# A shorter plan for the second attention: 12 phases instead of 15, and its scaling on another engine

## The reference, cut to what matters

```python
h = rms_norm(x, mix_norm_g); proj = h @ w_in          # q, kv (3 branches), gate logits, conv input
k_cmp = compress_tokens(kv[:, :, 0, 0], ...)          # silu(flat @ w1) @ w2 on overlapping blocks of 32 tokens
v_cmp = compress_tokens(kv[:, :, 0, 1], ...)
# three attentions with a bias by distance: compressed keys, selected blocks, window of 512
p = masked_softmax(s + bias, valid)                   # each of the three
out = gc[..., 0:1] * o_cmp + gc[..., 1:2] * o_sel + gc[..., 2:3] * o_win
conv = silu(layer_norm(causal_depthwise_conv(a * sigmoid(gate), 31 taps)))
x = x + concatenate([attn, conv]) @ w_out
```

## Time and profile before

| what | us |
|---|---|
| median of 3 runs (range) | 2780.38 (2778.89 to 2782.11) |
| the profiled execution | 2782.15 |
| its span, first to last instruction | 2780.0 |
| TensorE busy | 2725.3 (98%) |
| VectorE busy | 1945.8 (70%) |
| ScalarE busy | 1405.2 (51%) |

### The profile page before, as it was taken

How to read it: one execution, slowest core, us unless ns; L and a number is a source line. 1 busy time by engine, 2 the same in 40 slices (tenths; PEclk the granted TensorE clock), 3 DMA queues, 4 the chain that set the end, 5 groups by cost and what they waited for, 6 DMA issues and landing times. The chain is left out here.

```text
span 2780.0 us, 41613 instructions
## 1 busy us (share of the span) xinstructions
PE 2725.3 (98%) x16606; PEld 2393.7 (86%) x16606; DVE 1945.8 (70%) x2922; ACT 1405.2 (51%) x2084; POOL 101.0 (4%) x189
## 2 busy tenths in 40 slices
PE   8999999999999999999999998998999999999998
PEld 7888888888888888888888898988888888888887
DVE  7448777757777775677666777876788775677765
ACT  6335555544455554455454551247555553455543
POOL 1320000000000000000000000000000000000000
PEclk9999999999999999999999999999999999999999
DMA  7457556555668788878656566762355556555554
GB/s 239 134 172 241 175 182 196 184 182 190 198 225 286 283 278 301 284 274 285 209 171 208 177 203 229 247 251 92 126 178 190 194 192 189 180 192 196 183 193 140
DMA packets 166609, 573.19 MB, mean 206 GB/s; under 512 B 19872, under 2 KB 26736, under 8 KB 165904
## 3 DMA queue, kind: packets, MB, share of 16 engines
q1 hardware_dynamic: 151216, 521.86, 56.5%
q0 software_dynamic: 15056, 48.65, 4.7%
q10 hardware_dynamic: 144, 0.01, 0.0%
HBM read 530.86 MB, written 38.90 MB: 205 GB/s over the span
## 5 line engine op out<-in xcount | busy, mean ns | idle before, releaser
L1902 DVE TENSOR_TENSOR wl<-raw,wh 128x1024 fp32r<-128x1024 f32 (+1 forms) x880 | 1029.3, 1195 | 448.5 <-ACT wh L1359 446.3
L1359 ACT ACTIVATE wh<-raw 128x1024 fp32r<-128x1024 f32 (+1 forms) x880 | 885.9, 1031 | 507.6 <-PE PS L947 420.0
L947 PE MATMUL PS<-CHt,wh 128*128 128x512 f32 x2816 | 886.1, 396 | 2.2 <-DVE wl L1902 2.2
L947 PE MATMUL PS<-BIGt,wh 128*128 128x512 f32 (+1 forms) x2816 | 756.9, 356 | 3.1 <-DVE wl L1902 2.0
L947 PEld LDWEIGHTS PS<-CHt,wl 128*128 128x128 f32 x2816 | 529.0, 188 | 124.8
L947 PE MATMUL PS<-AHt,wh 128*128 128x512 f32 (+1 forms) x1984 | 603.2, 385 | 12.0 <-DVE wl L1902 9.4
L947 PE MATMUL PS<-CHt,wl 128*128 128x256 f32 x2816 | 553.5, 278 | 0.0
L947 PEld LDWEIGHTS PS<-BIGt,wl 128*128 128x128 f32 x2304 | 435.5, 189 | 79.1 <-issue 0.2
L947 PE MATMUL PS<-BIGt,wl 128*128 128x256 f32 x2304 | 498.3, 279 | 0.0
L947 PEld LDWEIGHTS PS<-BIGt,wh 128*128 128x128 f32 x2816 | 435.1, 190 | 8.5 <-issue 5.2
L947 PEld LDWEIGHTS PS<-CHt,wh 128*128 128x128 f32 x2816 | 429.3, 189 | 2.7 <-issue 2.5
(11 more groups left out here) (307 smaller groups left out, 1659.0 us busy)
## 6 DMA issues: line engine op xcount, KB each, us to landing
raw<-in_w_up SPq DMA_DIRECT2D x264, 512.0 KB, 4.8
raw<-in_w_in SPq DMA_DIRECT2D x200, 512.0 KB, 4.0
raw<-in_w_down SPq DMA_DIRECT2D x132, 512.0 KB, 4.3
raw<-in_w_gate SPq DMA_DIRECT2D x88, 512.0 KB, 5.4
raw<-in_w_down SPq DMA_DIRECT2D x56, 384.0 KB, 3.5
raw<-in_w_ssd_br SPq DMA_DIRECT2D x32, 512.0 KB, 4.4
raw<-in_w_o SPq DMA_DIRECT2D x32, 512.0 KB, 4.2
PKR<-in_w_in SPq DMA_DIRECT2D x32, 512.0 KB, 5.4
```

Of the source, the lines that this page charges most:

```text
L947: return e.matmul(o, l, r, start=start, stop=stop, skip_group_check=True)
L1359: return e.activation(o, x, f, **k)
L1902: return e.tensor_tensor(o, x, y, op)
```

## The change

Three things change together. First, `ATTN2` has other numbers: 12 phases instead of 15. With 12 + 1 steps a stage, pairs 0 and 1 run in steps 1 to 12 and 3 to 14, and both are over before query unit 1 is finished (step 16). So pairs 2 and 3 start in the same step 17, pairs 4 and 5 in step 30, and 6 and 7 in step 43, and the parts of both stand side by side in each step, even pair first. The last one ends in step 54. Second, the four scalings of each branch go from ScalarE (phase `p0`/`p1`) to VectorE (in `scale`, phase `r0`/`r1`, right behind the reciprocals), and the transposes wait for VectorE instead. Third, phases 1 and 2 of each compression stage stand two pieces later: behind pieces 579 and 580 (key), 587 and 588 (value).

```diff
-ATTN2 = dict(sc0=0, cmp=2, tr0=5, o0=6, sc1=7, trc=10, oc=12, tr1=12, o1=14, s0=0, ca=2, r0=2, cb=5, s1=7, r1=9,
-             out=14, e0=2, ce=3, p0=3, t0=5, e1=9, tc=10, p1=10, t1=12)
+ATTN2 = dict(sc0=0, cmp=2, tr0=3, o0=5, sc1=5, trc=7, oc=8, tr1=8, o1=10, s0=0, ca=2, r0=2, cb=4, s1=5, r1=7,
+             out=11, e0=1, ce=3, t0=4, e1=6, tc=7, t1=9)
...
-            add("w_in_2", 0, 16, 1024 + 256 * i, "U2", "ev_cmp", i, gens=[("compress", i, [0, None, None, 1, 2])], **k)
+            add("w_in_2", 0, 16, 1024 + 256 * i, "U2", "ev_cmp", i, gens=[("compress", i, [0, None, None, None, None, 1, 2])], **k)
...
             if ph == ATTN2["tr0"]:
                 bank7("tr0")
-                e.wait_ge(ac.sem, ac.at(i, "p03"))
+                e.wait_ge(d.sem, d.at(i, "p03"))
                 e.wait_ge(d.sem, d.at(i, "cb1"))
...
             if ph == ATTN2["tr1"]:
                 bank7("tr1")
-                e.wait_ge(ac.sem, ac.at(i, "p13"))
+                e.wait_ge(d.sem, d.at(i, "p13"))
...
-            def scale(br):
-                e.wait_ge(d.sem, d.at(i, f"rg{br}1"))
-                for hh in range(2):
-                    for b, c0, c1 in HALVES:
-                        x = SX[:, hh, c0:c1]
-                        af(x, x, ACT.Copy, scale=RC[:, hh, b:b + 1]).then_inc(ac.sem)
...
                 for hh in range(2):
                     tt(RC[:, hh, :], RC[:, hh, :], GAT[:, :, 3 * (2 * t + hh) + 1 + br], MUL).then_inc(d.sem)
+                e.wait_ge(d.sem, d.at(i, f"rg{br}1"))
+                for hh in range(2):
+                    for b, c0, c1 in HALVES:
+                        x = SX[:, hh, c0:c1]
+                        ts(x, x, RC[:, hh, b:b + 1], None, MUL).then_inc(d.sem)
```

More of the change, by code:

```diff
@@ L710, in hybrid_block_kernel @@
     a2_d = [steps(f"attn2_d{u}", "n000", "n010", "n100", "n110", "cb0", "cb1", "cm", "cs0", "cs1", "cf", "rc0", "rg00",
[L711 to L714, removed]
+                  "rg01", *[f"p0{j}" for j in range(4)], "cd", "cr", "cc", "cg0", "cg1", "cx0", "cx1", "n001", "n011", "n101", "n111", "rc1", "rg10",
+                  "rg11", *[f"p1{j}" for j in range(4)]) for u in range(2)]
+    a2_a = [steps(f"attn2_a{u}", *[f"e0{i}" for i in range(4)], "ce", "pt0", *[f"e1{i}" for i in range(4)], "ptc", "pt1") for u in range(2)]
     add_d = steps("conv_half_added")
@@ L1764, in attn2 @@
                 af(SC[:, :, :, :], SC[:, :, :, :], ACT.Exp).then_inc(ac.sem)
-            if ph == ATTN2["p0"]:
-                scale(0)
             if ph == ATTN2["t0"]:
@@ L1774, in attn2 @@
                 af(PT[0:15, :, 0:256], PS[0:15, S0:S0 + 2, 0:256], ACT.Copy).then_inc(ac.sem)
-            if ph == ATTN2["p1"]:
-                scale(1)
             if ph == ATTN2["t1"]:
```

## The result

| kernel | median us (range, runs) | profiled execution | its span | mean clock |
|---|---|---|---|---|
| before | 2779.97 (2778.89 to 2782.11, 4) | 2782.15 | 2780.0 | 0.995 |
| after | 2797.51 (2796.26 to 2797.88, 4) | 2797.88 | 2796.1 | 0.990 |

The ratio is 1.0059 (95% interval 1.0047 to 1.0071): slower by 17.5 us. The forecast was 2791.0, +10.8. The sign was right and the time lies in the range of 2777 to 2802, but 0.5 us beyond the forecast's own range of 2785 to 2797; the clock rival's 2800 is nearer.

The account below looks back on a forecast made before the run. TensorE was taken as the bound, busy 2725.3 of 2780.0 us. Compression +3.7 and attention +7.1 (20.4 of waits plus 1.5 for clock, against 11.5 + 3.3) made +10.8: 2791.0 us, range 2777 to 2802.

Parts of the forecast that it names:

- the clock rival: TensorE: each wait of 3 us or more is followed by the lower clock level, +9, 2800 us; chance 19%.
- -0.8 for the clock: TensorE: +1 for piece 581 at half clock, +1.5 behind attention waits, against 3.3 lost before.
- Compression, forecast +3.7: Key and value products: token waits of 4.7 + 6.2 us replaced by 13.6 for halves and GCM, plus 1 for clock.
- the prediction's own list: Signs it is wrong: GCM before 582's split, 583's fetch earlier than 1683, or no transpose waits in pairs 4 to 7.
- Scaling, forecast 1.0 us a branch: Attention's four scalings on VectorE: 354 and 290 ns less 70 ns overlap each; bounds 0.75 and 1.4 us.
- Waits of the attention, forecast 20.4 us: TensorE's waits in lock step by pairs of pairs: 4.4 + 6 + 5 + 5 us, against 11.5 before.
- a lower clock behind one or two of them: Attention: 1.5 us for TensorE's lower clock behind one or two waits, against 3.3 before.
- The key product hidden as meant: Compression: VectorE isn't blocked, only the value side's 5.7 us go, 2781.6 us, no change; chance 8%.
- ScalarE as the bound: Stretch 1852 to 1907: ScalarE was the bound, a pair of pairs costs 1.5 instead of 5, 2776 us; chance 13%.
- Waits near half of mine: Waits near half of those forecast: 2783 to 2785 us, no change; chance 10%.

Follow-up runs that it names:

- attn_stagger: Changed kernel with the compression's phases as before and odd pairs two steps behind even ones, still 12 phases: 2785.65 us, +4.4 against before.
- scale_dve: Kernel before with only the scaling of the probabilities moved to VectorE, 15 phases and compression as before: 2781.52 us, ratio 0.9998.
- comp_only: Kernel before with only the compression's phases 1 and 2 two pieces later, key and value side: 2784.32 us, +3.0.
- key_one: Kernel before with the compression's key side one piece later and its value side two: 2783.09 us, ratio 1.0009.
- attn_only: Changed kernel with the compression's phases where they were before, so 12 phases, lock step and VectorE's scaling alone: 2795.85 us, +14.5 against before.
- fill_elsewhere: attn_only plus 43 useless TensorE products, all ahead of pair 7's last value product, behind its wait: 2804.22 us, +22.9 against before.
- fill_half: attn_only plus 43 useless TensorE products ahead of its waits for the scaled probabilities: 2787.18 us, +6.3 against before.
- lock_act: Kernel before with 12 phases and both pairs in step as in the change, ScalarE still scaling, compression as before: 2799.89 us, +18.5.
- bias_late: Kernel before with the value side's phases two pieces later and the attention's bias load issued one unit later: 2777.62 us, ratio 0.9988.
- value_fill: Kernel before with the value side's phases two pieces later, plus 48 useless products ahead of its four longest waits: 2777.96 us, ratio 0.9987.

## Why the prediction was right in sign and short in size

**The sum.** The forecast's +10.8 is +11.6 of waits (2.7 in the compression, 20.4 - 11.5 in the attention) and -0.8 for the clock (+1, and 1.5 - 3.3). The profiles show +6.2 of idle time and +9.9 of slowed work. So the waits came at about half of what was forecast, and the slowed work came on top where the forecast had almost none. That 2797.5 lies in the range is in part luck: one error covered half of the other.

**Compression, forecast +3.7, measured +3.0.** The waits came where they were put and for what was named; their size did not. TensorE and VectorE in the changed kernel:

```profile
1681.58 0.79 PE L946 MATMUL PS<-BIGt,wh 128*128 128x256 f32 x2 [5.64 <-DMA wl<-parked_halves]
...
1697.35 0.48 PE L946 MATMUL PS<-GCM,W2C 64*64 64x64 f32 x4 [4.35 <-DVE GCM L1894]
```

```profile
1689.05 1.23 DVE L1890 TENSOR_TENSOR wl<-raw,wh 128x1024 fp32r<-128x1024 f32 x1 [8.50 <-ACT wh L1358]
...
1697.11 0.19 DVE L1894 TENSOR_SCALAR GCM<-GCM 64x64 f32<-64x64 f32 x1
```

TensorE stands still for 5.6 + 4.4 = 10.0 us (forecast 13.6), against 11.0 in the earlier trace rows. GCM is made behind the split of piece 582 and two tap phases, as worked out, at 1697.3 (forecast 1699.3). The 2 us come from the fetch of piece 583, for which the prediction took the 1683.54 of the earlier trace rows. It went out at 1681.55 (the first of six in this line), which by the prediction's own list speaks against it:

```profile
1681.55 17.83 SPq L791 DMA_DIRECT2D raw<-in_w_in  x6
```

The runs don't show that the change moved it. SyncE was ahead by then through one issue that starts at 1664.5, and the plans differ only from 1673 on; first before, then after:

```profile
1664.65 7.89 SPq L789 DMA_DIRECT2D wh<-parked_halves  x1
```

```profile
1664.50 5.83 SPq L788 DMA_DIRECT2D wh<-parked_halves  x1
```

And with the compression of before, the same fetch went out at 1682.10 in attn_stagger and at 1681.25 in scale_dve. So the prediction read to 0.01 us a time that differs by 2 us between executions. By the waits the compression should then have won 1.0. What took that back, and 3 us more, is slowed work, which I had at +1: comp_only has 1.1 us less of idle time and 3.1 more of busy time, and the windows at 1680 and 1696 of the changed kernel are granted 0.50. A part of the 3.1 may lie in the attention (5.4 us of clock missing there against 3.3). The reason given for +1 had a misreading in it: the key product of the earlier trace rows was no example of the upper level (before has 0.72 and 0.86 in the windows from 1676 to 1684). At 1.00 it takes 3.72 us, as in key_one, against 3.77, so the conclusion holds, for that product alone. The two errors cancelled, and +3.7 near +3.0 is luck. Of the meant gain of 11 us, half can be had: the value side alone gives 5.8 (value_later), and the key side has no better place among the three measured.

**Scaling, forecast 1.0 us a branch, measured 1.01** (four in a run; 347 ns for 256 columns and 284 for 128, where 354 was read from the earlier trace rows and 290 estimated). The overlap is 84 ns for each, not 70; the six taps (2.38 us for 6 x 479 ns) give 82 to 99.

**Waits of the attention, forecast 20.4 us, measured 17.4.** TensorE in the changed kernel, the larger waits of pairs 0 and 1 (two lines), 2 and 3 (three), 4 and 5 (one), 6 and 7 (two):

```profile
1825.90 0.87 PE L1275 MATMUL PS<-M,SX2a 128*128 128x128 f32 x6 [1.32 <-DVE SX2a L1894]
...
1838.97 1.15 PE L946 MATMUL PS<-PT2b,VN 128*64 128x128 f32 x12 [1.89 <-ACT PT2b L1358]
...
1870.27 0.87 PE L1275 MATMUL PS<-M,SX2a 128*128 128x128 f32 x6 [1.64 <-DVE SX2a L1894]
...
1872.65 1.37 PE L1275 MATMUL PS<-M,SX2b 128*128 128x128 f32 x6 [1.51 <-DVE SX2b L1894]
...
1888.64 0.61 PE L1331 MATMUL PS<-M,SCMb 128*15 128x128 f32 x4 [2.54 <-DVE CC L1890]
...
1919.97 0.92 PE L1275 MATMUL PS<-M,SX2b 128*128 128x128 f32 x6 [1.51 <-DVE SX2b L1894]
...
1959.22 1.54 PE L1275 MATMUL PS<-M,SX2a 128*128 128x128 f32 x6 [3.10 <-DVE SX2a L1894]
...
1961.61 1.54 PE L1275 MATMUL PS<-M,SX2b 128*128 128x128 f32 x6 [0.85 <-DVE SX2b L1894]
```

With the smaller ones, by pairs of pairs: 3.8 (forecast 4.4), 5.7 (6), 3.9 (5), 4.0 (5). In three of the four each stands where it was put and waits for what was named: the chain through bias, exponentials, the split and the scalings was read rightly from rows of before. In pairs 4 and 5 the first transposes waited 0.5 us and not 2.2, and a wait of 0.9 in the second branch was not foreseen.

**The term that failed: the clock behind these waits.** The prediction has "plus 1.5 for a lower clock behind one or two of them". It was set against 3.3 of before, so the forecast had the clock *gain* 1.8 us. By the sums of waits alone the attention would be 17.4 - 11.5 = +5.9; it is +14.5. In the profiled execution the missing clock of the attention went from 3.3 to 14.9 us, and TensorE's own work of the whole span grew by 9.9. Six transposes, 0.87 us at the upper level, took 1.37 and 1.54 behind such waits (above), and 8 us without any wait ran at 0.50. The forecast gave a lower level to one or two of the waits, and its clock rival to those of 3 us or more; here it fell behind waits of 1.5 to 2.5 as well, so every pair of pairs from 2 and 3 on had it. The length of a single wait doesn't tell it: attn_stagger has waits of up to 2.8 us, and 1.00 and 0.98. That waits close together are what lowers it is my reading of these windows; no run moves the same waits apart. And nearly the same waits cost different amounts in different executions: the clock missing is 10.2 us in attn_only, 13.8 in fill_elsewhere, 14.9 after. Taking fill_half against fill_elsewhere, the clock's share of such waits is 6 us; by the medians of fill_half and attn_only it is up to 8.

**The rivals.** The key product hidden as meant (8%): no, 5.6 and 4.4 us of waits. ScalarE as the bound (13%): the PT2a waits did go, and lock_act suggests that VectorE's scaling is worth some 4 us in step (the intervals overlap), but the waits of a pair of pairs are 4 to 5.7, not 1.5. Waits near half of mine (10%): in the attention they were 85% of it; with the compression's the added idle time was near half (6.2 of 11.6), but the slowed work kept the time from 2785. The clock rival (19%) had the missing part right and 2800 for the time, with one condition wrong, the 3 us.

**Which step makes the loss.** The prediction did not separate shorter distances from lock step. The stagger does: 12 phases alone cost 4, lock step 10. I read it as the same chain seen twice: two pairs that ask for VectorE and ScalarE in the same half piece make two waits a transpose apart, while two steps of distance put other pieces' products between them.

Open: what made the tokens' DMAs take longer in bias_late, and why the same waits lose more clock in one execution than in the next. It may be what makes attn_only's four executions span 4.4 us; only the quickest has a profile, and no clock is missing there in block one.

## What to carry to other kernels

On a TensorE-bound kernel price a wait twice: its length, and the work behind it at half the clock. Short waits close together can cost as much again as they add up to (here +6.2 us of idle time and +9.9 of slowed work). When the busy time of the same instructions differs between two profiles, the clock is what to look at. An overlapped schedule should keep the partners apart, by steps in which the engine has other work. And when one engine's step is moved by a piece, look at what then stands in front of it in *every other* engine's queue: in key_one one place behind a blocked split cost 9.5 us.

The fastest kernel measured is value_later, 2775.0 us, 5.8 below the kernel before: only the value side's two phases are later.

## What the runs showed of the hardware that was not expected

- 43 useless products ahead of waits made attn_only 8 us faster (2795.85 to 2787.18); the same 43 without a wait behind them made it 8 us slower (2804.22).
- The granted level fell behind waits of 1.5 to 2.5 us each, and stayed at 0.50 for 8 us in which TensorE was busy throughout (1892 to 1900).
- A 128x128 product in fp32 is two instructions here, 0.24 us at the upper level and 0.41 at the lower (16 instructions in 3.28 us in value_fill, in a window at 0.67). Transposes of the same shape and type are one each.
- The same wait cost clock in one execution and none in another. In block one, in the same code, TensorE waits 1.74 us for VectorE near 472 us in before as in fill_half; the windows of 4 us from 472 on then show 1.00 and 1.00 in before, 0.92 and 0.65 in fill_half.
- VectorE's scaling by a per-partition scalar in place, fp32: 347 ns for 128x256, 284 ns for 128x128, four in a run in 1.01 us; ScalarE's same four take 1.50.
